# Post-norm joints by the root, dealt modulation products, and a reordered second attention in a two-block transformer with experts

## The reference

```python
# first block, twice: retention mixer, then sparse attention (NSA) with shared keys and values
h = h + rms_norm(mixed, mix_norm_post[layer])
normed = rms_norm(h, ffn_norm_pre[layer])
h = h + rms_norm(swiglu_ffn(normed, w_in, w_out), ffn_norm_post[layer])
# rms_norm(x, g) = x * rsqrt(mean(x * x) + 1e-6) * g
```

## Time and profile before

| What | us |
|---|---|
| Runs shown | 1993.4, 1990.33, 1993.21 |
| Median | 1993.21 |
| Span of the profiled execution | 1988.3 (no separate time of it is recorded; 4.9 below the median) |
| TensorE busy (share of span) | 1601.5 (81%) |
| VectorE busy | 754.2 (38%) |
| ScalarE busy | 557.1 (28%) |
| POOL busy | 114.2 (6%) |
| DMA | 604.31 MB, mean 304 GB/s |

### The profile page before, as it was taken

How to read it: one execution, slowest core, us unless ns; L and a number is a source line. 1 busy time by engine, 2 the same in 40 slices (tenths; PEclk the granted TensorE clock), 3 DMA queues, 4 the chain that set the end, 5 groups by cost and what they waited for, 6 DMA issues and landing times.

```text
span 1988.3 us, 26400 instructions
## 1 busy us (share of the span) xinstructions
PE 1601.5 (81%) x11487; PEld 1134.5 (57%) x11487; DVE 754.2 (38%) x1094; ACT 557.1 (28%) x878; POOL 114.2 (6%) x100
## 2 busy tenths in 40 slices
PE   7999999999899999999999855566555556555556
PEld 7899999998679999897798311111111111111112
DVE  6766767675648555668655100000000000000000
ACT  4454544354754344436653000000000000000001
POOL 1101000000313000003300000000000000000000
PEclk9999999999999999999999988777878777778878
DMA  9854597648165555353278999999999999999997
GB/s 353 300 176 161 136 312 259 225 159 273 57 262 193 194 185 169 127 172 105 86 275 346 420 432 432 432 431 430 431 431 432 431 432 432 431 431 432 429 430 315
DMA packets 100521, 604.31 MB, mean 304 GB/s; under 512 B 5340, under 2 KB 60821, under 8 KB 75336
## 3 DMA queue, kind: packets, MB, share of 16 engines
q1 hardware_dynamic: 91456, 587.22, 73.7%
q10 hardware_dynamic: 7832, 11.26, 1.9%
q0 software_dynamic: 1136, 4.40, 1.6%
HBM read 595.52 MB, written 4.20 MB: 302 GB/s over the span
## 4 chain that ended last, share of the span: by engine, by line
PE 55%; DMA 38%; DVE 4%; ACT 1%; issue 1%; POOL 0%; DVEq 0%; ACTq 0%
DMA _expert_slots_and_tokens<-in_experts 38%; PE ps L772 19%; PE ps L841 13%; PE ps L1469 4%; PE ps L826 3%; PE ps L1288 2%; PE ps L1503 2%; PE ps L794 2%; DVE split_operands L649 1%; PE ps L1051 1%; PE ps L1321 1%; PE ps L1428 1%; PE ps L1311 1%; ACT split_operands L641 1%; PE ps L1064 0%
## 5 line engine op out<-in xcount | busy, mean ns | idle before, releaser
L772 PE MATMUL ps<-split_operands 128*128 128x256 f32 x3360 | 412.2, 284 | 3.1 <-DVE split_operands L649 1.9
L649 DVE TENSOR_TENSOR split_operands<-dense_ring_and_tables,split_operands 128x1024 fp32r<-128x1024 f32 x282 | 343.5, 1260 | 178.5 <-ACT split_operands L641 178.3
L772 PEld LDWEIGHTS ps<-split_operands 128*128 128x128 f32 x3360 | 406.4, 192 | 6.3 <-issue 3.3
L641 ACT ACTIVATE split_operands<-dense_ring_and_tables 128x1024 fp32r<-128x1024 f32 x284 | 284.5, 1050 | 301.8 <-PE ps L772 156.5
L2724 DVE TENSOR_TENSOR arena<-arena,ps 128x512 f32<-128x512 f32 x16 | 11.0, 688 | 570.9 <-PE ps L1469 570.9
L1993 ACT ACTIVATE arena<-ps 128x512 f32<-128x512 f32 x16 | 9.6, 597 | 565.0 <-PE ps L1469 565.0
L841 PE MATMUL ps<-split_operands 128*128 128x256 f32 x1248 | 152.0, 284 | 2.7 <-DVE split_operands L679 2.7
L841 PEld LDWEIGHTS ps<-split_operands 128*128 128x128 f32 x1248 | 150.3, 192 | 4.7 <-DVE split_operands L679 3.5
L841 PE MATMUL ps<-hidden_split,split_operands 128*128 128x256 f32 x960 | 118.6, 283 | 0.8 <-DVE split_operands L649 0.8
L841 PEld LDWEIGHTS ps<-hidden_split,split_operands 128*128 128x128 f32 x960 | 116.6, 192 | 1.0 <-DVE split_operands L649 1.0
L1469 PE MATMUL ps<-_expert_slots_and_tokens,arena 128*32 128x512 f32 x400 | 70.5, 868 | 58.0 <-DMA _expert_slots_and_tokens<-in_experts 58.0
(11 more groups left out here) (361 smaller groups left out, 1781.6 us busy)
## 6 DMA issues: line engine op xcount, KB each, us to landing
dense_ring_and_tables<-in_experts SPq DMA_DIRECT2D x36, 4096.0 KB, 43.2
_expert_slots_and_tokens<-in_experts SPq DMA_DIRECT2D x35, 4096.0 KB, 43.1
arena<-in_experts SPq DMA_DIRECT2D x17, 4096.0 KB, 43.1
dense_ring_and_tables<-in_ffn_units SPq DMA_DIRECT2D x66, 1024.0 KB, 4.9
dense_ring_and_tables<-in_ret_w_in SPq DMA_DIRECT2D x23, 1024.0 KB, 8.1
dense_ring_and_tables<-in_w_in SPq DMA_DIRECT2D x22, 1024.0 KB, 5.1
dense_ring_and_tables<-in_w_ada SPq DMA_DIRECT2D x12, 1024.0 KB, 6.9
arena<-in_experts SPq DMA_DIRECT2D x6, 2048.0 KB, 8.4
```

The source lines that it names most:

```text
L641: act.activation(w_hi[:, n % 2, c], ring[U % RING][:, c], ACT.Copy).then_inc(hi_ready, 1)
L649: dve.tensor_tensor(w_lo[:, n % 2, c], ring[U % RING][:, c], w_hi[:, n % 2, c], ALU.subtract).then_inc(lo_ready, 1)
L772: mm = pe.matmul(ps[:, bank, b * T:b * T + T], left, right, start=k == 0 and i == 0, stop=k == 7 and i == 2)
```

## The change

Five parts. (1) The four joints: h is multiplied by the root and the gained output is added, so that h is over-scaled by the root; the next norm takes eps times root squared in place of eps through one product more; a later reciprocal (`root_inverse`) and two multiplications (`over_root`) put h right. The last two chunks are squared singly, VectorE copies quarter 0 of the next unit's high half, ScalarE makes quarters 2 and 3 after the root; ten fillers after joint 1 go, and 14 become 10 after joint 2. POSTF1 becomes a joint like the others, and POOL's split goes. (2) `mod_norm` interleaves scaling, shift and low half; a quarter of the context's value products goes ahead of N_IN2, whose squares are summed first; `wide_tok` runs over k outside and t inside. (3) First attention: another order of turned heads, compressed turn, the four `ada` products and the copies. (4) Second attention: masking and maximum apart, head 0's factors ahead of head 1's maximum, `rotate_q(3)` later, Exp's table loaded ahead, the first copy ahead of the third exponential, the last head copied by two engines. (5) Tail: `merge(0)` and the pair's low half ahead of `product_b(1)`.

The diff, cut to its core:

```diff
+RS_NO = {N_PRE0: 0, N_PREF0: 1, N_PRE1: 2, N_PREF1: 3, N_IN2: 4}
+POST_NO = {N_POST0: 0, N_POSTF0: 1, N_POST1: 2, N_POSTF1: 3}
+AFTER_POST = {N_PREF0: 0, N_PRE1: 1, N_PREF1: 2, N_IN2: 3}
...
-        JOINTS = {N_POST0: U_F0 + 1, N_POSTF0: U_KV + 1, N_POST1: U_F1 + 1}
+        JOINTS = {N_POST0: U_F0 + 1, N_POSTF0: U_KV + 1, N_POST1: U_F1 + 1, N_POSTF1: U_IN2 + 1}
...
             def norm(n):
-                for q in ADDED.get(n, range(4)):
-                    if n in ADDED and q == 0:
+                if n in AFTER_POST:
+                    pe.wait_ge(eps_ready, AFTER_POST[n] + 1)
+                    pe.matmul(ps[:, SUM_BANK[n], 0:T], ones[:], eps_r2, start=True, stop=False)
+                for q in ADDED[n]:
+                    if q == 0:
                         pe.wait_ge(sq_added, 2 * n + 2)
...
             norm(N_POST0)
             pe.wait_ge(on_ev, 4)
             bias_table(0)
-            warm(10, 1, 0)
...
             bias_table(1)
-            warm(14, 1, 0)
+            warm(10, 1, 0)
...
+            def n_turn(hd, fill=0):
...
+                warm(fill, 4, 384)
+                pe.wait_ge(s_p, hd + 1)
...
             cmp_scores(1)
-            n_turn(4)
+            n_turn(4, 4)
             n_scores(4)
             n_values(1)
+            cmp_turn(1)
             n_turn(5)
             n_values(2)
             n_scores(5)
             n_turn(6)
-            cmp_turn(1)
+            ada(0)
             n_turn(7)
+            ada(1)
             n_values(3)
             n_scores(6)
             n_turn(8)
+            ada(2)
             n_turn(9)
-            ada(0)
-            ada(1)
             n_turn(10)
             n_scores(7)
             n_values(4)
-            ada(2)
+            n_turn(11)
             ada(3)
-            n_turn(11)
...
             keys(ctxn, 7).then_inc(ctx_mm, 1)
+            take(U_V)
+            values(ctxn, 6, 0, range(4))
             norm(N_IN2)
-            take(U_V)
-            values(ctxn, 6).then_inc(ctx_mm, 1)
+            values(ctxn, 6, 0, range(4, 8))
+            values(ctxn, 6, 1, range(8)).then_inc(ctx_mm, 1)
...
+                taken(act, last)
+                for c in (6, 7):
+                    act.activation(sq[:, c, :], acc_chunk(ACC[n], c), ACT.Square).then_inc((sq_half, sq_ready)[c % 2], 1)
+                quarter_hi_split(act, U + 1, 1)
                 roots(n)
+                for i in (2, 3):
+                    quarter_hi_split(act, U + 1, i)
...
+            def root_inverse():
+                dve.reciprocal(rs_post, root[:]).then_inc(dve_step, 1)
...
+            def over_root(told, half):
+                dve.wait_ge(dve_step, told)
+                c = h[:, 4 * half:4 * half + 4, :]
+                ins = dve.tensor_tensor(c, c, rs_post.unsqueeze(1).to_broadcast([P, 4, T]), ALU.mult)
+                if half:
+                    ins.then_inc(h_true, 1)
...
                 for k in range(10 if next_name else 9):
                     if k < 8:
-                        dve.scalar_tensor_tensor(out=xn[:, k, :], in0=acc_chunk(ACC[n], k), scalar=col(name, k),
-                                                 in1=rs[:], op0=ALU.mult, op1=ALU.mult).then_inc(scaled, 1)
+                        steps[0] += 1
+                        dve.tensor_tensor(xn[:, k, :], h[:, k, :], root[:], ALU.mult).then_inc(dve_step, 1)
                     if 1 <= k < 9:
-                        dve.wait_ge(scaled, POST[n] + k)
-                        dve.tensor_tensor(h[:, k - 1, :], h[:, k - 1, :], xn[:, k - 1, :],
-                                          ALU.add).then_inc(h_ready, 1)
+                        dve.wait_ge(dve_step, steps[0] - (k < 8))
+                        dve.scalar_tensor_tensor(out=h[:, k - 1, :], in0=acc_chunk(ACC[n], k - 1), scalar=col(name, k - 1),
+                                                 in1=xn[:, k - 1, :], op0=ALU.mult, op1=ALU.add).then_inc(h_ready, 1)
...
+                dve.scalar_tensor_tensor(out=eps_r2, in0=root[:], scalar=EPS * D / P, in1=root[:], op0=ALU.mult,
+                                         op1=ALU.mult).then_inc(eps_ready, 1)
...
-            w_max(0)
-            w_max(1)
-            rotate_q(3)
+            w_mask(0)
+            w_neg(0)
+            w_mask(1)
+            w_factors(0)
+            w_neg(1)
+            split_lo(dve, U_G + 1)
+            w_factors(1)
...
             product_b(0)
+            merge(0)
+            split_lo(dve, U_PB + 4)
+            pair_lo(dve, X_WO, 0, two_chunks(gb, 0))
             product_b(1)
-            merge(0)
             product_b(2)
             merge(1)
-            pair_lo(dve, X_WO, 0, two_chunks(gb, 0))
...
-            split_lo(pool, U_IN2 + 1)
```

More of the change, by code:

```diff
@@ L1229, in keys, with values @@
                 return mm
-            def values(src, bank):
-                for t in range(2):
-                    for k in range(8):
-                        mm = pe.matmul(ps[:, bank, t * T:t * T + T], src[:, k, t * P:t * P + P],
-                                       slot8(U_V)[:, k, :], start=k == 0, stop=k == 7)
+            def values(src, bank, t, ks):
+                for k in ks:
+                    mm = pe.matmul(ps[:, bank, t * T:t * T + T], src[:, k, t * P:t * P + P],
+                                   slot8(U_V)[:, k, :], start=k == 0, stop=k == 7)
                 return mm
@@ L1531, in roots @@
                 act.wait_ge(ss_ready, n + 1)
-                if n:
-                    act.wait_ge(rs_ready, n)
-                act.activation(root[:], ps[:, SUM_BANK[n], 0:T], ACT.Sqrt, scale=1.0 / D,
-                               bias=EPS).then_inc(root_ready, 1)
+                if n in POST_NO:
+                    if POST_NO[n]:
+                        act.wait_ge(h_true, POST_NO[n])
+                    act.activation(root[:], ps[:, SUM_BANK[n], 0:T], ACT.Sqrt, scale=1.0 / D,
+                                   bias=EPS).then_inc(root_ready, 1)
+                else:
+                    act.activation(rs[:], ps[:, SUM_BANK[n], 0:T], ACT.Sqrt, scale=1.0 / D,
+                                   bias=0.0 if n in AFTER_POST else EPS).then_inc(root_ready, 1)
             def of_h(q):
@@ L1639, in post @@
                     act.wait_ge(landed[(U + 1) % RING], 16 * ((U + 1) // RING + 1))
-                for q in range(4):
-                    if q < 3:
-                        act.wait_ge(acc_done, TOLD[n] + q + 1)
-                    else:
-                        taken(act, last)
-                        if n in JOINTS:
-                            quarter_hi_split(act, U + 1, 0)
+                for q in range(3):
+                    act.wait_ge(acc_done, TOLD[n] + q + 1)
                     act.activation(sq[:, 2 * q:2 * q + 2, :],
@@ L1942, in _ @@
                     gate_out(p)
+                if hd == 0:
+                    w_pout(0)
                 if hd + 2 < HEADS:
                     w_exp(hd + 2)
-                w_pout(hd)
-                if hd % 2 == 0:
-                    split_hi(act, U_G + 2 + p if p < 6 else U_PA + p - 6)
+                if 0 < hd < 15:
+                    w_pout(hd)
+                if hd % 2 == 0 and p < 7:
+                    split_hi(act, U_G + 2 + p if p < 6 else U_PA)
+            act.wait_ge(s_tr, 2 * HEADS)
+            act.activation(w_pT(15)[:, 2:4, :], ps[:, 1, :].rearrange("p (k t) -> p k t", k=2), ACT.Copy).then_inc(s_trev, 1)
             for u in range(4):
@@ L2617, in _ @@
                 gated(ga, 0, b)
-            for u in range(3):
+            for u in range(2):
                 split_lo(dve, U_PB + 2 + u)
```

163 lines of the change are left out of this document (96 added, 67 removed).

## The result

The changed kernel takes 1974.76 us (median of five runs, 1974.04 to 1976.58), the kernel before 1991.09 beside it: a ratio of 0.9914 [0.9902, 0.9926], 16.3 us less. 1977.3 was forecast, with a range of 1973.0 to 1984.5. A second set of runs of the changed kernel gave 1974.43 against 1989.91, a ratio of 0.9919 [0.9906, 0.9933].

What follows compares the result with a forecast made beforehand. Experts are bound by the weight stream, the dense part before by TensorE; the stream follows the dense end. Joints 7.85, first attention 3.1, second 2.7 and 2.0, tail 0.25: 15.9 off 1993.2 gives 1977.3 us, range 1973.0 to 1984.5.

Steps and rivals of the forecast that it cites:

- tail: Output projection: a merged pair's low half, for which the first unit waits 1.45, comes sooner; 0.25 us gained (0 to 1.15).
- second attention: Start: head 0's factors no longer wait for head 1's maximum, 2.7 us; end: two engines share the last head's copy, 2.0.
- joint 4: Two norms in a row: second root 1.5 us sooner, interleaved scaling and low half 1.6, less 0.1; 3.0 gained (1.5 to 5).
- joints 1 to 3: Layer output normed and added: root sooner and reciprocal off the path; gains of 2.4, 2.1 and 1.3 us.
- first attention: New order of turned heads and modulation products fills TensorE's rest and avoids the half-clock stretch; 3.1 us gained (0 to 7).
- 0.75 for the earlier root: Joints: last square in two pieces and a quarter copied by VectorE bring the root 0.75 us sooner.
- The statistic's extra product: Three following norms each get one more product, for eps times root squared, with nothing to hide it; 0.75 us lost.
- The correction of h: VectorE's later reciprocal and two multiplications, 4.2 us four times, mostly covered by its idle time; 0.2 us lost.
- my own sign of being wrong: Wrong if over-scaled h makes a unit wait, the attention shows a half-clock stretch, or the expert stream stays put.
- first rival: First attention: the clock falls all the same, only later, so the 3.1 us is gone; 1980.4 us, chance 0.30.
- The stream does not follow: Expert weights: SP's order of issue fixes the stream, so no dense-part saving reaches the end; 1992 us, chance 0.05.
- slower rival: Four joints and second attention's start: without fillers the clock falls, 3.4 us each, slower from four stretches; 1997.4 us, chance 0.03.

Runs made afterwards that it cites:

- e12: Changed kernel with three fillers in joint 1, seven for ten in joint 2, third modulation product behind head 9, five fillers ahead of heads 10 and 12: 1974.03 us.
- e3: Changed kernel with the first attention's order as before on TensorE, ScalarE and VectorE: 1979.2 us, ratio 0.9943.
- e7: Changed kernel with joint 4's second norm in the old order, eight scalings first, then shift and low half by chunk: 1975.88 us.
- e8: Changed kernel with all of the context's value products behind joint 4's second norm, as before; squares still summed first: 1974.45 us.
- e6: Changed kernel with the first attention's four modulation products dealt as before, everything else as changed: 1974.87 us, ratio 0.9918.
- e5: Changed kernel with the first attention's order as before on TensorE and ScalarE, as changed on VectorE alone: 1974.93 us, ratio 0.9916.
- e11: Changed kernel with VectorE's order at the second attention's start as before: 1976.78 us, ratio 0.9934.
- e10: Changed kernel with the ten fillers behind joint 1 as before the change: 1976.2 us.
- e1: Changed kernel with three fillers behind the bias table of joint 1: 1973.96 us, ratio 0.9912.
- e4: Changed kernel with the third modulation product behind turned head 9 in place of head 8: 1974.15 us.
- e9: The changed kernel itself once more, nothing altered: 1974.43 us.
- e2: Kernel before the change without its ten fillers behind joint 1, nothing else altered: 1992.53 us against 1991.44, ratio 1.0006.

## Why the prediction was right, and where its steps were not

**Time and direction** came out as forecast: 16.3 us against 15.9, by the mechanism named, work taken off or moved off the path of TensorE's waits. That the sum is so close is in part luck: errors of both signs cancel. Costs of 0.95 that I took off did not come (steps 2 and 3), and the tail gave 0.35 more, the second attention's start 0.3 and joint 4 0.2; joints 1 to 3 gave 0.6 less, the second attention's end 0.5 and the first attention 0.2. Together that is the 0.5 between 15.9 and the ledger's 16.4. The 1977.3 lies 2.5 above the 1974.76, and 2.1 of that is the base: the median of before was 1993.21 in the three runs that I had and 1991.09 in the five. No run undoes the change of joints 1 to 3 by itself; their gain is read from stretches in which all profiles agree.

1. *Joints 1 to 3*: 2.2, 1.9 and 1.1 against 2.4, 2.1 and 1.3. The term that was too high in all three is the 0.75 for the earlier root. From the statistic's first product to the root it was 2.39 in the profile of before and is 2.03 now, so 0.4. The rest of each joint gave 0.2 back. In joint 1 (root to product 4.60, now 2.75) it is the reciprocal's 1.75 and another 0.1, where I had taken 0.1 off. That fillers end last in joint 2 and small products in joint 3 was right, and e12 confirmed the 0.3 in joint 2.
2. *The statistic's extra product*, −0.75, measured 0.0: joint 1 to 2 is 191.72 in both kernels at full clock, and the two stretches behind joints 2 and 3 are alike too. The product is dearer than the 0.25 that I gave it, 0.43 from its start to the next (237.85 to 238.28), but I was wrong that there is nothing to hide it: the unit behind waits for its own low half, which comes no later than before. It starts 12.97 us behind the joint's first product in both. The kernel before (first product at 227.90), and e3 (at 226.24):

```profile
240.86 11.75 PE L772 MATMUL ps<-split_operands 128*128 128x256 f32 x96 [0.33 <-DVE split_operands L649]
```

```profile
237.85 0.59 PE L749 MATMUL ps<-_expert_slots_and_tokens,ones 128*128 128x256 f32 x2
238.28 1.03 PE L758 MATMUL ps<-_expert_slots_and_tokens,ones 128*128 128x256 f32 x4
239.21 11.74 PE L782 MATMUL ps<-split_operands 128*128 128x256 f32 x96
```

3. *The correction of h*, −0.2, measured 0: 1.75 and 2 x 1.22 us of VectorE in each of four places, and the stretches of TensorE that hold them are as long as before.
4. *Joint 4*: 3.2 against 3.0. The two halves that I gave it, 1.5 for an earlier root and 1.6 for the interleaving, are ends of one tie. TensorE's values ended at 809.1 before and the weight product began at 809.01, so the interleaving alone would have won nothing there; now the values end at 801.04 and the first low half at 800.91. e7 shows the interleaving's 1.6 and e8 the 0.7 of the moved values, each real because the other side was brought down too. Most of TensorE's side is the second norm: ten passes (eight of squares, two of the eps product) without a wait in place of sixteen with three waits of 0.39, 0.32 and 0.32.
5. *First attention*: 2.9 of stretch at full clock against 3.1, 1.8 in both profiles of the changed kernel, and 5 us by the medians of e3. The sign and place were right, the reason at most half: I took the dealt products as what fills the rest, and e6 shows that it does as well without dealing them; e5 points to VectorE's order, one copy ahead of a low half. That this wait was behind a low half was in the trace (the 2.14 of the earlier trace rows is released by VectorE, whose row just ahead of the copy is a low half of 2.36) and I did not look at what stood ahead of the copy.
6. *Second attention*: 3.0 against 2.7 at the start, 1.5 against 2.0 at the end. The cause at the start was named wrongly in the main. I looked for 3.0 us in place of 5.7 between the second masking and the first turned head; it is 4.95 (893.54 to 898.49). The larger part lies ahead of it: the masking itself comes 2.2 sooner behind the first scores, since a low half of 2.35 us moved behind it, as e11 shows. In TensorE's terms the waits of 2.31 and 0.63 of the earlier trace rows are gone. *Tail*: 0.6 against 0.25; the wait fell by 1.0 (1.45 to 0.45), and 0.4 of it was lost again on the way to the router.

**The rivals.** By my own sign of being wrong, a half stretch in the attention, the first rival has a part in the result: the clock did fall there in both profiles of the changed kernel, for 3.4 us and at a price of 1.2, not 3.1, and in e10, with the same attention, for 10.2 us and 4.4; but not in e1, e7, e8 and e11 with the same attention, nor in e4. Its time, 1980.4, did not come. "The stream does not follow" is out: the first expert transfer behind the seam was issued 13.05 us sooner, and the rest of the program took 902.1 and 902.6 us. The slower rival had its mechanism at one joint (a fall behind joint 1, 1.5 us) and, 41 us behind joint 2, in the keys and values (1.6), and was far from the four that it needed. The rule of the Trainium skill ("TensorE: Matmul & The Clock Gate", Part 4: PE-mode transpose) that a transpose does not count as a busy TensorE in the same way is neither borne out nor refuted: the stretches that fell in the attention hold transposes, but so do the same stretches where it did not fall, and the fall behind joint 1 has none ahead of it.

## What to carry to other kernels

Look at what stands ahead of a small copy or reciprocal on its engine before looking at the engine that waits: the wait of 2.3 us in the second attention, and by all signs that of 2.1 in the first, came from a unit's low half that stood ahead of a short instruction. Where two engines reach a point together, neither's saving shows alone, so cost them together. Fillers belong only into waits that are there in every execution; in a wait that is sometimes shorter they are the last to end. And judge a fall of the clock by several executions, since one profile may catch none or three, and compare how the executions started before you put a fall down to an edit.

## What the runs showed that was not expected

With the same code up to joint 1 and no fillers behind it, nine profiles (the changed kernel twice, e3 to e8 and e11) differ only in when joint 1's statistic starts. In the six that started at 219.78 to 220.12 the clock fell behind it, and in e8, e11 and e3, at 220.74, 220.67 and 221.47, it did not:

```profile
225.00:228.50 3.50, 2.99 (x25) 2.99 (x26) 3.50 (x11) 2.61 (x6) 0.00 (x0) 1.00 0.00 0
```

The three kernels with fillers lie at 220.94 to 221.34, where none fell anyway, so whether fillers hold the clock in the changed kernel stays open. Behind joint 2 the same code fell in three profiles (statistic of joint 1 at 220.02, 219.80, 219.78), though not in e7, at 220.00.

The traces show where the drift comes from: all of it lies in the first 20 us. TensorE's first 48 weight products and the first norm behind them, in the changed kernel and in e8:

```profile
10.02 7.56 PE L882 MATMUL ps<-split_operands 128*128 128x256 f32 x48 [10.02 <-DVE split_operands L2131]
17.42 1.02 PE L758 MATMUL ps<-_expert_slots_and_tokens,ones 128*128 128x256 f32 x4
9.85 8.46 PE L882 MATMUL ps<-split_operands 128*128 128x256 f32 x48 [9.85 <-DVE split_operands L2130]
18.15 1.02 PE L758 MATMUL ps<-_expert_slots_and_tokens,ones 128*128 128x256 f32 x4
```

From this norm to joint 1's statistic are 202.6 us in every profile. What differs is the start of the 48 products (9.70 to 10.53) and how long they take. That length sorts all fourteen profiles. At 7.38 to 7.56 (after, e6, e9) the clock fell behind joint 1 and in the keys and values; at 7.66 to 7.89 (e4, e5, e7, and e2 with the old code) behind joint 1 alone; at 8.46 to 8.68 (the other seven, the kernel before among them) at neither. Between 14 and 16 us TensorE ran 19 products in the first profile and 14 in e8. So an execution that is 0.5 to 1.7 us sooner at joint 1 pays 1.5 or 3.1 behind it, and a single profile's span is off by 1.2 to 1.6 us for each short fall. The falls in the attention do not follow this order (e10 fell at 8.53, e1 at 8.58 did not), and why the first products take longer in one execution than in another is open.
